# Where the low part of the weights is made: VectorE's subtraction, or a negated copy and an accumulating DMA

## The reference

```python
mod = c_act @ w_ada + b_ada;  shift, scale, gate = split(mod, 3)
h = rms_norm(x, g_norm) * (1 + scale) + shift
proj = h @ w_in                                  # 1024 x 7168
u = v * sigmoid(gv);  y = depthwise_conv(u, 31 taps) + b_dw
y_a = (silu(layer_norm(y)) * silu(z)) @ w_a_out
p = causal_means(u_b, windows 2, 4, 8, 16) - u_b
y_b = (group_matmul(p, w_grp) * p_scale * silu(z_b)) @ w_b_out
m = sigmoid(proj_a) * y_a + sigmoid(proj_b) * y_b
y = rms_norm(x + gate * (m @ w_out), g_final)
```

## Time and profile before

| | |
|---|---|
| median of 3 runs | 995.64 us |
| profiled execution: its time | 995.86 us |
| profiled execution: span of the trace | 993.7 us |
| TensorE matmul busy | 971.8 us (98%), 6196 instructions |
| VectorE busy | 694.6 us (70%) |
| ScalarE busy | 252.7 us (25%) |
| GpSimd busy | 1.9 us |
| HBM traffic | 106 GB/s over the span |
| TensorE's share of the chain that ended last | 96% |

### The profile page before, as it was taken

One profiled execution on the slowest core, in us unless ns is written; L12 is line 12 of the kernel. 1 busy time (PEld: TensorE's weight loads), 2 busy tenths in 40 slices (PEclk: granted clock), 3 DMA queues, 4 the chain that ended last, 5 costly groups with the idle time before them and its releaser, 6 DMA issues.

```text
span 993.7 us, 14662 instructions
## 1 busy us (share of the span) xinstructions
PE 971.8 (98%) x6196; PEld 958.9 (97%) x6196; DVE 694.6 (70%) x687; ACT 252.7 (25%) x264; POOL 1.9 (0%) x12
## 2 busy tenths in 40 slices
PE   4999999999999999999999999999999999999997
PEld 3799999999999999999999999999999998999996
DVE  6878988627898772889864689978788743342346
ACT  5531112221122221111222111122633512122242
POOL 0000000000000000000000000000000000000000
PEclk9999999999999999999999999999999999999998
DMA  9611221231131231222024112213871173125104
GB/s 376 246 43 56 95 81 54 85 122 44 64 111 34 86 117 58 64 86 97 27 75 143 43 66 100 65 54 123 320 283 63 30 310 128 44 87 190 43 1 170
DMA packets 31960, 106.39 MB, mean 107 GB/s; under 512 B 7712, under 2 KB 14112, under 8 KB 28448
## 3 DMA queue, kind: packets, MB, share of 16 engines
q1 hardware_dynamic: 28304, 92.82, 26.8%
q10 hardware_dynamic: 3600, 12.72, 3.3%
HBM read 82.74 MB, written 22.79 MB: 106 GB/s over the span
## 4 chain that ended last, share of the span: by engine, by line
PE 96%; DVE 1%; DMA 1%; ACT 1%; SPq 0%; issue 0%; DVEq 0%
PE ps L463 31%; PE ps L466 31%; PE ps L464 31%; DMA bf<-x_t 1%; PE aux L415 1%; DVE stage_hi L886 1%; PE aux L449 0%; PE aux L421 0%; DVE hf L1159 0%; ACT hf L710 0%; PE aux L635 0%; PE aux L627 0%; ACT w_hi L678 0%; ACT L716 0%; SPq L302 0%; DVE bf L900 0%
## 5 line engine op out<-in xcount | busy, mean ns | idle before, releaser
L464 PE MATMUL ps<-hr,w_hi 128*128 128x344 f32 x1536 | 486.7, 320 | 0.0
L463 PE MATMUL ps<-hr,w_hi 128*128 128x344 f32 x1344 | 426.4, 320 | 0.0
L928 DVE SCALAR_TENSOR_TENSOR conv_y<-conv_u,par,conv_y 128x1024 f32<-128x1024 f32 x240 | 308.0, 1283 | 20.6 <-PE ps L466 14.1
L464 PEld LDWEIGHTS ps<-hr,w_hi 128*128 128x128 f32 x1536 | 288.9, 188 | 0.0
L466 PE MATMUL ps<-hr,w_lo 128*128 128x344 f32 x1344 | 285.0, 320 | 0.0
L463 PEld LDWEIGHTS ps<-hr,w_hi 128*128 128x128 f32 x1344 | 252.7, 188 | 1.7 <-issue 1.7
L466 PEld LDWEIGHTS ps<-hr,w_lo 128*128 128x128 f32 x1344 | 224.7, 188 | 0.0
L678 ACT ACTIVATE w_hi<-w_raw 128x1024 fp32r<-128x1024 f32 (+1 forms) x88 | 87.5, 996 | 270.8 <-PE ps L466 270.8
L862 DVE TENSOR_TENSOR w_lo<-w_raw,w_hi 128x1024 fp32r<-128x1024 f32 (+1 forms) x88 | 101.2, 1150 | 52.0 <-ACT w_hi L678 46.7
L463 PE MATMUL ps<-gr,w_hi 128*128 128x344 f32 x384 | 123.3, 323 | 0.0
L464 PE MATMUL ps<-gr,w_hi 128*128 128x344 f32 x384 | 121.8, 320 | 0.0
(11 more groups left out here) (128 smaller groups left out, 590.8 us busy)
## 6 DMA issues: line engine op xcount, KB each, us to landing
w_raw<-w_main SPq DMA_DIRECT2D x80, 512.0 KB, 3.6
ada_raw<-w_ada SPq DMA_DIRECT2D x8, 1024.0 KB, 16.9
bf<-x_t SPq DMA_DIRECT2D x4, 1032.0 KB, 8.6
sig_a<-stage_lo ACTq DMA_DIRECT2D x8, 516.0 KB, 2.7
sig_b<-stage_hi ACTq DMA_DIRECT2D x8, 516.0 KB, 2.6
y_conv<-conv_y SPq DMA_DIRECT2D x8, 516.0 KB, 2.9
silu_z<-stage_hi ACTq DMA_DIRECT2D x8, 516.0 KB, 4.2
bf<-y_conv SPq DMA_DIRECT2D x4, 1032.0 KB, 6.9
```

The costliest lines, as they stand in the source:

```text
L463: nc.tensor.matmul(out, wh, rhs_hi[:, cols(c)], start=(k == 0), stop=False)
L464: nc.tensor.matmul(out, wh, rhs_lo[:, cols(c)], start=False, stop=False)
L928: return v.scalar_tensor_tensor(out=y, in0=conv_u[:, x, k:k + SEQ], scalar=par[:, x, k:k + 1], in1=y, op0=ALU.mult, op1=ALU.add)
```

## The change

`w_lo` of jobs 2 to 87 is made in another way. ScalarE writes, right behind `w_hi`, a second copy of `w_raw` with scale -1 into `w_lo`, which rounds to minus the hi part, and raises `w_neg_done`. GpSimd waits for that and issues a DMA that adds `w_raw` onto `w_lo`, SBUF to SBUF; its landing is counted per slot (`lo_landed`). TensorE and SyncE wait for the landing instead of `w_lo_done`. VectorE's subtractions go, but for those of jobs 0 and 1. SyncE's loop over the pairs is written out, and TensorE gets one wait per pair that the old order implied.

```diff
+        def wait_lo(engine, s):
+            if s < 2:
+                engine.wait_ge(w_lo_done, s + 1)
+            else:
+                engine.wait_ge(lo_landed[s % 2], 16 * (s // 2))
@@ sync
-            with sp.Fori(0, PAIRS) as g:
+            for g in range(PAIRS):
...
                 for i in range(JOBS_PER_PAIR):
-                    sp.wait_ge(w_lo_done, g * JOBS_PER_PAIR + (i + 1))
+                    wait_lo(sp, g * JOBS_PER_PAIR + i)
...
             def load_main(s):
-                sp.wait_ge(w_lo_done, s - 1)
+                wait_lo(sp, s - 2)
@@ gpsimd
+            for s in range(2, JOBS):
+                n = weight_columns(s) if s < PAIR_TOTAL else KT * P
+                pool.wait_ge(w_neg_done, s - 1)
+                pool.dma_start(w_lo[:, s % 2, 0:n], w_raw[:, s % 2, 0:n], accum_op=ALU.add).then_inc(lo_landed[s % 2], 16)
@@ tensor
-                pe.wait_ge(w_lo_done, g * JOBS_PER_PAIR + (i + 1))
+                wait_lo(pe, g * JOBS_PER_PAIR + i)
...
                     pe.wait_ge(act_evac, g * ACT_EVACS + (i + 1))
+                    if i == 0 and g > 0:
+                        pe.wait_ge(dve_evac, g * DVE_EVACS)
@@ scalar
-            def split_hi(slot, n, loaded):
+            def split_hi(slot, n, loaded, first=False):
                 act.wait_ge(raw_full[slot], loaded)
                 nc.scalar.activation(w_hi[:, slot, 0:n], w_raw[:, slot, 0:n], ACT.Copy).then_inc(w_hi_done, 1)
+                if not first:
+                    nc.scalar.activation(w_lo[:, slot, 0:n], w_raw[:, slot, 0:n], ACT.Copy, scale=-1.0).then_inc(w_neg_done, 1)
@@ vector
-                def split():
-                    split_lo(i % 2, weight_columns(i + 2), g * JOBS_PER_PAIR + (i + 3))
...
-            def split_for(s):
-                if s + 2 < JOBS:
-                    split_lo(s % 2, KT * P, s + 3)
```

More of the change, by code:

```diff
@@ L255, in build @@
         w_lo_done = sem("w_lo_done")
+        w_neg_done = sem("w_neg_done")
+        lo_landed = [sem("lo_landed0"), sem("lo_landed1")]
         pe_done = sem("pe_done")
@@ L295, in build, with weight_columns @@
         LINKS = 1 + 2 * (1 + (2 + CONV_W) + (DOUBLINGS + 2 + 1))
+        def wait_lo(engine, s):
[3 more added lines that the diff above has]
+                engine.wait_ge(lo_landed[s % 2], 16 * (s // 2))
+        def weight_columns(i):
+            return MIX_WIDTH if PAIR_JOBS[i % JOBS_PER_PAIR][0] == "pool_mix" else KT * P
         block = ctx.enter_context(nc.Block())
@@ L563, in job_pairs @@
                 for s in range(first, first + count):
-                    pe.wait_ge(w_lo_done, s + 1)
+                    wait_lo(pe, s)
                     pe.wait_ge(dve_evac, PAIRS * DVE_EVACS + s - 1 - JOB_B)
@@ L669, in _ @@
             spread(2)
-        def weight_columns(i):
-            return MIX_WIDTH if PAIR_JOBS[i % JOBS_PER_PAIR][0] == "pool_mix" else KT * P
         @block.scalar
         def _(act):
-            def split_hi(slot, n, loaded):
+            def split_hi(slot, n, loaded, first=False):
                 act.wait_ge(raw_full[slot], loaded)
                 nc.scalar.activation(w_hi[:, slot, 0:n], w_raw[:, slot, 0:n], ACT.Copy).then_inc(w_hi_done, 1)
+                if not first:
+                    nc.scalar.activation(w_lo[:, slot, 0:n], w_raw[:, slot, 0:n], ACT.Copy, scale=-1.0).then_inc(w_neg_done, 1)
             act.dma_start(c_in[:], t["c_t"]).then_inc(c_loaded, 16)
@@ L711, in _ @@
             for s in range(2):
-                split_hi(s, KT * P, 16)
+                split_hi(s, KT * P, 16, first=True)
             for c in range(CHUNKS):
@@ L949, in taps, with pool_tile @@
                     tap_at[0] += 1
-            def pool_tile(g, x, split):
+            def pool_tile(g, x):
                 u = pool_u[:, x, :]
@@ L959, in pool_tile @@
                                                 scalar=poolc[:, n:n + 1], in1=src[:, POOL_MAX:POOL_MAX + SEQ], op0=ALU.mult, op1=ALU.add))
-                    if n == 0:
-                        split()
                 full = sig[:]
@@ L1018, in pair_step @@
                     v.tensor_copy(ext_pool[:, tile, POOL_BUF, :], pool_u[:, tile, POOL_MAX + SEQ:POOL_MAX + TOK]).then_inc(u_ready, 1)
-                    pool_tile(g, tile, split)
+                    pool_tile(g, tile)
                 if i == 10:
                     pool_lo(g, 1)
-                if i not in (8, 9):
-                    split()
                 taps(g, after)
@@ L1058, in _ @@
                     merge_b(0)
-                    split_for(JOB_B)
             for e in range(1, KT):
@@ L1065, in _ @@
                     merge_b(1)
-                    split_for(JOB_B + 1)
             merge_b(2)
-            split_for(JOB_B + 2)
             for c in range(CHUNKS):
@@ L1075, in _ @@
                     merge_b(3)
-                    split_for(JOB_B + 3)
                 last = v.tensor_tensor(bf[:, e, :], bf[:, e, :], row_rstd, ALU.mult)
@@ L1085, in _ @@
                     merge_b(4 + e // 2)
-                    split_for(JOB_B + 4 + e // 2)
                 dve.wait_ge(a_hi_done, e + 1)
@@ L1090, in _ @@
             merge_b(7)
-            split_for(JOB_B + 7)
             for m in range(KT):
@@ L1100, in _ @@
                 v.tensor_tensor(m_row, t_row, m_row, ALU.add).then_inc(m_full, 1)
-                split_for(s)
                 dve.wait_ge(m_hi_done, m + 1)
@@ L1129, in _ @@
                 dve.sem_inc(x_new_ready, 1)
-                split_for(JOB_OUT + m)
                 if m >= 1:
```

## The result

The changed kernel takes 1071.29 us (median of 4, 1070.35 to 1072.6) against 995.54 for the kernel before: a ratio of 1.0762 (95% interval 1.0743 to 1.0780), 75.8 us slower. Forecast were 1066 and a range of 1023 to 1110.

What follows compares the result with a forecast made beforehand. TensorE was taken as the bound: 993.7 us of span plus 54.5 of waits for the landing and 16 for the clock gave 1064.2 us of span, hence a time of 1066 us. The range was 1023 to 1110.

Steps and rivals of the forecast that it cites:

- TensorE is the bound, VectorE's relief is worth 0: Whole kernel: removing 98.8 us of VectorE subtractions gains 0, since TensorE waits for none of it.
- The place: jobs 13 and 15 of each pair, job 2, the last product: Where cover is short, ten TensorE waits for w_lo's landing, 4.5 to 5.5 us each.
- x = 6.0: Time in us from the negation's end to the landing TensorE sees: a load's 3.6, second read 1.4, GpSimd's work 0.96.
- The estimate from the Trainium skill, 4.4 us: Negation's end to landing from two pages: 2.0 us plus 1.05 MB over 436 GB/s; waits would sum to 37 us.
- x - 0.54: Wait at jobs 13 and 15 of a pair: time from negation's end to landing, less 0.54 us, eight times.
- Product 6 of w_b_out waits 1.4: At that product, hi part held back by LayerNorm work on ScalarE, TensorE waits 1.4 us for w_lo's landing.
- The clock: Behind ten waits of 4.5 to 5.5 us the granted clock mostly falls: 1.6 us each, 16 us together.
- rival A: TensorE's clock holds through the waits: 1050 us; chance 0.23.
- Rival B: The adding DMA takes longer than 8.2 us and every product waits: about 1200 us; chance 0.13.
- C: The add is hardly dearer than a store, landing after about 3 us, waits of 2.5: 1019 to 1025; chance 0.09.
- D: Not slower: at jobs 13 and 15 the add lands inside the margin, below 0.54 us: 995.6 us; chance 0.03.

Runs made afterwards that it cites:

- e8: Changed kernel with VectorE's subtraction at jobs 0, 1, 2, 13, 15 (mod 16) and in all last 24 products; 44 accumulating DMAs stay: 996.01 us, ratio 0.9999.
- e1: Changed kernel with w_lo of jobs 13 and 15 of each pair made by VectorE's subtraction again: 1020.56 us, ratio 1.0246.
- e6: Changed kernel with a plain GpSimd DMA in place of the accumulating one, so the lo part isn't computed: 1029.28 us, ratio 1.0338.
- e7: Kernel before with ScalarE's negated copy, VectorE adding w_raw onto it in place of its subtraction, no GpSimd DMA: 1003.74 us, ratio 1.0077.
- e4b: Changed kernel with ScalarE's negated copy ahead of the hi part; TensorE and SyncE wait for both: 1059.26 us, ratio 1.0644.
- e3b: Changed kernel with 17 and 22 small unused matmuls ahead of TensorE's waits at jobs 13 and 15: 1060.93 us, ratio 1.0646.
- e3: Changed kernel with 32 and 40 small unused matmuls ahead of TensorE's waits at jobs 13 and 15, which outlasted the waits: 1080.67 us, ratio 1.0858.
- e2: Changed kernel with VectorE making w_lo wherever that kernel waits and at job 1 of each pair; 67 accumulating DMAs stay: 1003.03 us, ratio 1.0079.
- e5: Changed kernel with the silu_z store of tile 0 issued one product later in the first three pairs: 1069.06 us, ratio 1.0732.

## Why the prediction was right, point by point

- **TensorE is the bound, VectorE's relief is worth 0.** Right: e8 relieves VectorE of 43 us and moves nothing. (Of TensorE's waits at the end the 0.2 us one is at 984 us, not behind 985.)
- **The place: jobs 13 and 15 of each pair, job 2, the last product.** Right. Forecast were 43.7 us at jobs 13 and 15, measured 4.1 at each job 13 and 5.2, 5.2, 5.2 and 6.6 at jobs 15, 38.6 together; at job 2 4.9 were forecast and 4.7 measured, at the last product 4.5 and 3.1. e1 takes the eight away and gets 51 us back.
- **x = 6.0.** Too long by 1.1 where the DMA runs alone (4.9). Beside the store it is 6.0, but the prediction had no store in its sum: that it fits there is luck. Of its terms, GpSimd's 0.96 was 0.86, and the second read, with the 0.34 more on GpSimd, 1.7 for 1.4; but a plain DMA from GpSimd, SBUF to SBUF, lands in 2.9 with GpSimd's 0.53 in it, not in a load's 3.6 with 0.96 on top. The estimate from the Trainium skill, 4.4 us (DMA: Bandwidth & Descriptors, Anatomy of one DMA, with Collectives: The Full Stack, The bandwidth ceiling), was nearer to the 4.6 us of the profile, and the rule of the second page that an add costs a second read (written of the adding step of a collective) agrees with the 1.7 us of e6. With 4.4 the waits would have summed to 37 us, though, further from the 52.4 measured than my 54.5: it is the time of a DMA alone, and more than half of these ran beside a store or loads.
- **The formula, x - 0.54.** It holds once x is known: at job 13 an x of 4.9 gives 4.3 us, and the list's 4.1 with the 0.2 that it doesn't show is 4.3; e7 gave 0.60 for 0.7, e6 2.4 for 2.7. What I didn't foresee is x beside other traffic: at jobs 15 I expected about 1 us more in e4b and 3.8 in e6, and the waits were 3.1 and 2.4: in e4b the store follows the DMA later, and the shorter DMA of e6 isn't held up by it.
- **Product 6 of w_b_out waits 1.4.** Wrong: it did not wait. Three others did, 6.0 us together (1.97, 1.42, 2.58: products 1 and 4 of w_b_out, 1 of w_a_out), because the accumulating DMA runs there beside megabytes of loads. I had checked whether the loads are late, not whether they delay the new DMA. In the stretch of the first:

```profile
bf<-y_conv SPq DMA_DIRECT2D x1, 1032.0 KB, 12.8
w_lo<-w_raw POOLq DMA_DIRECT2D x1, 512.0 KB, 11.8
```

- **The clock.** Right in kind (rival A falls: e3b), somewhat small: 11 dips at 13 waits. The matmuls' 23.9 us, less 13 x 0.23 for the restarts, is 20.9, 1.9 a dip; I had 1.6 at ten places, 16. The dips differ: the product costs 1.6 us more where the clock falls after the restart, 2.5 at job 13 of the first pair and 2.9 at job 2 (15.4 us from its first matmul to the next hi part, 12.6 before), where most of the dip falls on work. The rule of the Trainium skill that activity releases the clock (TensorE: Matmul & The Clock Gate, What's actually happening) is borne out by e3b, where matmuls without use hold it at 1.00 in all eight places.
- **Rival B (x over 8.2 everywhere).** The DMA took 12 us in single places, but at most 7.1 at jobs 13 and 15 of the changed kernel, and e8's 44 never made TensorE wait. C's x of about 3 is what a DMA without the add has (3.2 in e6), not one with it. D falls.

The sum came out 5 us low. The waits with their restarts are 55.4 us (52.4 and 3.0) for 54.5 forecast, the dips 20.9 for 16, and 0.7 is gone at the start. That the waits fit so well is in part luck: the eight at jobs 13 and 15 are 3.2 us shorter than forecast, the last product's 1.1 and that of product 6 1.4, and the three that I had not seen make up for it with 6.7. The place and the kind of the loss were forecast; the traffic beside the new DMA was not.

## What to carry to other kernels

What makes an operand ready is priced as a chain against the shortest cover in the schedule, not as load on an engine: DMAs of 4.6 us are free behind products of 11.4 us (44 of them in e8), and eight behind products of 2.8 us cost 51 us (e1). A DMA in place of an instruction brings in its latency (4.6 for 1.2 us) and whatever else runs on the DMA engines at that moment. If TensorE does have to rest for 4 us, useless matmuls in the gap keep its clock up (e3b: 10 us less for eight gaps), but only if they are counted so that they don't outlast it (e3: 9 us more); better, make those few operands by the quick way and the rest by the other.

## What the runs showed of the hardware

- An accumulating DMA of 128x1024 float32 within SBUF, from GpSimd, lands 4.6 us after its issue, a plain one 2.9; GpSimd is busy 0.86 and 0.53 us with them. Beside a 516 KB store issued 0.65 us behind it the adding one takes 5.7 us (4.5 if the store comes 1.60 us behind it, e4b), beside four loads of 1 MB 12 (e2).
- Of the waits of TensorE, those of 0.6 us left the granted clock at 1.00 (e7), one of seven of 2.4 us was followed by a fall and those of 3.0 and 3.3 us were not (e6), those of 3.1 us were in the later pairs but not in the first (e4b), and those of 4.1 us and more always in the changed kernel, though there two shorter ones (2.0 and 2.6) were too and the last (3.1) was not. In e4b one of 1.8 us was. So the length of a wait alone doesn't decide it. In the changed kernel the fall came up to 0.8 us after TensorE had resumed in five of the eleven.
- A product at which the clock has fallen took 1.6 to 2.9 us longer (13.2 and 14.1 for 11.6 at jobs 13, 15.4 for 12.6 at job 2).
- From about 33 us on the granted clock is 0.50 for a stretch in the profiles of e4b, e5, e7 and e8 and 1.00 in those of the other runs, though the work there is the same. In e8 the span is 1.3 us longer with it than that of the kernel before.
